# Token-major projections xv, hv and sv: from 1024 x 256 weight pieces to 512 x 512 pieces, in a fused two-block fp32 kernel

## The reference, cut to what matters

```python
# first block, cross-attention on the 256 memory rows
k, v = jnp.split(mem @ w_xkv, 2, axis=-1)          # xv: the v half, 1024 columns
o = jnp.einsum('bhsm,bmhd->bshd', pr, v)          # pr: softmax of q k, 4 heads of 256
# second block
proj = u @ w_in
hq, hf, hi, hg, sq, sk, sv = jnp.split(proj, splits, axis=-1)   # hv is hi, 512 columns; sv, 512 columns
o_hg = hgrn2_mix(hq, hf, hi, lb_all[i])                   # a decayed linear attention, hi as values
o_sb = stick_breaking_mix(sq, sk, sv)              # 8 heads of 64, sv as values
```

## Time and profile before

| | us |
|---|---|
| runs | 1045.93, 1047.46, 1048.79 (median 1047.46) |
| profiled execution, its own time | 1046.91 |
| its span in the trace | 1045.1 |
| PE busy | 990.6 |
| DVE busy | 626.1 |
| ACT busy | 514.2 |

### The profile page before, as it was taken

The page is one execution under the profiler, slowest core; times in us unless marked ns, Lnnn a source line. Parts: engine busy times, 40 slices in busy tenths (PEclk is TensorE's granted clock), DMA queues, the critical chain, the costliest instruction groups (busy, mean ns, idle before and its releaser), DMA issues.

```text
span 1045.1 us, 19430 instructions
## 1 busy us (share of the span) xinstructions
PE 990.6 (95%) x8574; PEld 914.9 (88%) x8574; DVE 626.1 (60%) x833; ACT 514.2 (49%) x693; POOL 19.6 (2%) x23
## 2 busy tenths in 40 slices
PE   7999999999999999999996777799999999999998
PEld 6999999899989999998674454499999999999998
DVE  6798789868676875444110110089984765555566
ACT  5576588834775573533111111177657554434453
POOL 0000021001000000000000000000000000000000
PEclk9999999999999999999998988899999999999999
DMA  7665453446235467788999999964421366455531
GB/s 290 243 236 183 187 190 134 161 162 224 99 125 206 154 220 279 316 353 334 423 418 421 420 420 421 419 221 162 162 82 52 124 242 239 168 196 202 200 124 42
DMA packets 34872, 241.76 MB, mean 231 GB/s; under 512 B 4064, under 2 KB 4448, under 8 KB 6368
## 3 DMA queue, kind: packets, MB, share of 16 engines
q1 hardware_dynamic: 33264, 233.32, 58.6%
q0 software_dynamic: 1232, 6.99, 1.8%
q10 hardware_dynamic: 288, 0.15, 0.1%
HBM read 239.36 MB, written 1.08 MB: 230 GB/s over the span
## 4 chain that ended last, share of the span: by engine, by line
PE 76%; DMA 12%; DVE 7%; ACT 2%; SPq 2%; issue 1%; DVEq 0%; ACTq 0%
PE ps L483 18%; PE ps L484 18%; PE ps L485 18%; DMA wr<-in_c_weights 8%; PE ps L572 3%; PE ps L1282 3%; DMA T8b<-in_c_weights 3%; SPq L3057 2%; DVE wlo L2048 2%; PE ps L969 1%; PE ps L1232 1%; DVE xs L2280 1%; ACT whi L1392 1%; PE ps L1309 1%; PE ps L856 1%
## 5 line engine op out<-in xcount | busy, mean ns | idle before, releaser
L2048 DVE TENSOR_TENSOR wlo<-raw,whi 128x2048 fp32r<-128x2048 f32 (+1 forms) x119 | 271.1, 2281 | 111.7 <-ACT whi L1392 111.3
L483 PE MATMUL ps<-XUh,whi 128*128 128x256 f32 x986 | 277.4, 281 | 0.5 <-DVE wlo L2048 0.4
L484 PE MATMUL ps<-XUl,whi 128*128 128x256 f32 x992 | 275.3, 277 | 0.0
L485 PE MATMUL ps<-XUh,wlo 128*128 128x256 f32 x992 | 274.9, 277 | 0.0
L1392 ACT ACTIVATE whi<-raw 128x2048 fp32r<-128x2048 f32 (+1 forms) x119 | 225.1, 1894 | 45.5 <-PE ps L485 39.0
L483 PEld LDWEIGHTS ps<-XUh,whi 128*128 128x128 f32 x986 | 185.5, 188 | 2.5 <-issue 1.7
L484 PEld LDWEIGHTS ps<-XUl,whi 128*128 128x128 f32 x992 | 186.6, 188 | 0.7 <-issue 0.5
L485 PEld LDWEIGHTS ps<-XUh,wlo 128*128 128x128 f32 x992 | 186.3, 188 | 0.0
L2980 DVE SCALAR_TENSOR_TENSOR sphs<-sphs,wsl,ps 128x256 f32<-128x256 f32 x8 | 3.8, 481 | 91.0 <-ACT sphs L2013 72.0
L483 PE MATMUL ps<-ffnah,whi 128*128 128x256 f32 x176 | 48.6, 276 | 0.0
L484 PE MATMUL ps<-ffnal,whi 128*128 128x256 f32 x176 | 48.6, 276 | 0.0
(11 more groups left out here) (626 smaller groups left out, 2377.9 us busy)
## 6 DMA issues: line engine op xcount, KB each, us to landing
raw<-in_c_weights SPq DMA_DIRECT2D x137, 1024.0 KB, 4.9
wr<-in_c_weights SPq DMA_DIRECT2D x36, 1024.0 KB, 26.1
xhi<-in_c_weights SPq DMA_DIRECT2D x12, 1024.0 KB, 26.2
xlo<-in_c_weights SPq DMA_DIRECT2D x12, 1024.0 KB, 26.4
extra<-in_c_weights SPq DMA_DIRECT2D x10, 1024.0 KB, 27.5
T<-in_c_weights SPq DMA_DIRECT2D x5, 1024.0 KB, 26.1
T8b<-in_c_weights SPq DMA_DIRECT2D x5, 1024.0 KB, 26.4
acb<-sums POOLq DMA_DIRECT2D x4, 1024.0 KB, 5.1
```

What stands on the lines that cost most here:

```text
L483: pe.matmul(ps, h(k), xh(k), start=start and k == 0, stop=False, skip_group_check=loose)
L484: pe.matmul(ps, h(k), xl(k), start=False, stop=False, skip_group_check=loose)
L485: t = pe.matmul(ps, l(k), xh(k), start=False, stop=stop and k == kt - 1, skip_group_check=loose)
L2048: dve.tensor_tensor(l[:, 0:n], r, h[:, 0:n].bitcast(F32), ALU.subtract).then_inc(*did("w_lo", "split", i))
```

## The change

`halved` makes pieces of 512 rows by 512 columns for xv, hv and sv; a piece is 1 MB as before, 4 row tiles of 128 x 512. Two pieces make one result of 512 columns. A product streams 512 columns. Each token tile has a bank of its own, which is held over both pieces; the first product of the even piece starts the sum and the last of the odd piece ends it. The two transposes ahead of xv are gone. ACT empties a pair of banks, 512 columns each, once the odd piece is through; for hv this is at the place of the old second `tokens`, and likewise for sv. In the second block hv and sv take banks 6 and 7 only, and scores, diagonal, z and rem rotate over banks 0 to 5 with a counter of their own, while sk, osb, oh, hg and the later users stay in the rotation over all eight.

```diff
@@ -183,6 +183,11 @@
         for c in range(c0, c0 + n, step):
             add(name, w, slice(c, c + step))
 
+    def halved(name, w, c0, n):
+        for c in range(c0, c0 + n, 512):
+            for k in (0, 512):
+                add(name, w[k:k + 512], slice(c, c + 512))
+
     w_in, w2, wgu, wdn = I["w_in"][0], I["w_in_2"][0], I["w_gate_up_2"][0], I["w_down_2"][0]
     add("dt", np.tile(w_in[:, 5120:5152], 4), slice(None))
     several("lora", w_in, 5152, 512)
@@ -205,7 +210,7 @@
     several("w_o", I["w_o"][0], 0, 1024)
     several("xk", I["w_xkv"][0], 0, 1024)
     several("xq", I["w_xq"][0], 0, 1024)
-    several("xv", I["w_xkv"][0], 1024, 1024)
+    halved("xv", I["w_xkv"][0], 1024, 1024)
     several("xo", I["w_xo"][0], 0, 1024)
 
     for g in range(8):
@@ -216,8 +221,8 @@
     several("hq", w2, 0, 512)
     several("sq", w2, 2048, 512)
     several("sk", w2, 2560, 512)
-    several("hv", w2, 1024, 512)
-    several("sv", w2, 3072, 512)
+    halved("hv", w2, 1024, 512)
+    halved("sv", w2, 3072, 512)
     several("hg", w2, 1536, 512)
     several("w_out2", I["w_out_2"][0], 0, 1024)
 
@@ -533,17 +538,19 @@
                     elif c == cs[0] and between is not None:
                         between()
 
-        def chunk_tok(name, c, xh, xl, kt, ready, banks=bank):
+        def chunk_tok(name, c, xh, xl, banks=bank, among=(0, 1, 2, 3, 4, 5, 6, 7)):
             i = first[name] + c
             h, l = split_of(i)
-            ps, free = banks.take(name, c)
-            w.wait_ge(*free)
+            if c % 2 == 0:
+                for j in range(2):
+                    _, free = banks.take(name, c // 2, j, among=among)
+                    w.wait_ge(*free)
             w.wait_ge(*at_("split", i))
-            if name == "xv" and c == 0:
-                lead_in(ps)
+            k0 = 4 * (c % 2)
             for j in range(2):
-                t = triple(ps[:, 256 * j:256 * j + 256], lambda k: xh[:, k, 128 * j:128 * j + 128], lambda k: xl[:, k, 128 * j:128 * j + 128],
-                           lambda k: h[:, k, :], lambda k: l[:, k, :], kt, ready)
+                f = slice(128 * j, 128 * j + 128)
+                t = triple(banks.ps(name, c // 2, j)[:, :], lambda k: xh[:, k0 + k, f], lambda k: xl[:, k0 + k, f],
+                           lambda k: h[:, k, :], lambda k: l[:, k, :], 4, start=k0 == 0, stop=k0 == 4)
             t.then_inc(*did("w_used", "used", i))
 
         def norm_sum(nm, nt, ng=1, banks=bank):
@@ -835,7 +842,7 @@
                 if r:
                     t.then_inc(*did("xa_pe", "xa_sc", j))
         for c in range(3):
-            chunk_tok("xv", c, MMh, MMl, 8, None)
+            chunk_tok("xv", c, MMh, MMl)
         for mj in range(2):
             for r in range(2):
                 ps, free = bank.take("xpT", mj, r)
@@ -845,12 +852,13 @@
                     for j in range(2):
                         t = pe.transpose(ps[:, 256 * a + 128 * j:256 * a + 128 * j + 128], Px[j][:, 2 * r + a, 128 * mj:128 * mj + 128], ident)
                 t.then_inc(*did("xa_pe", "xa_pT", mj, r))
-        chunk_tok("xv", 3, MMh, MMl, 8, None)
+        chunk_tok("xv", 3, MMh, MMl)
         for hd in range(4):
             ps, free = bank.take("xo_h", hd)
             w.wait_ge(*free)
             w.wait_ge(*at_("emptied", "xpT", 1, 1))
-            w.wait_ge(*at_("emptied", "xv", hd))
+            w.wait_ge(*at_("emptied", "xv", hd // 2, 0))
+            w.wait_ge(*at_("emptied", "xv", hd // 2, 1))
             for e in range(2):
                 for mj in range(2):
                     t = pe.matmul(ps[:, 256 * e:256 * e + 256], v2[:, mj, 256 * hd + 128 * e:256 * hd + 128 * e + 128], PXT[mj][:, hd, :],
@@ -955,14 +963,14 @@
             X = Xs[lv % 2]
             w.wait_ge(*at_("hg", "x", lv))
             if lv == 7:
-                ps, free = ebank.take("hsc", lv)
+                ps, free = ebank.take("hsc", lv, among=(0, 1, 2, 3, 4, 5))
                 w.wait_ge(*free)
                 for hd in range(4):
                     t = pe.matmul(ps[:, 128 * hd:128 * hd + 128], X[:, hd, 0:128], X[:, hd, 128:256])
                 t.then_inc(*did("hg_pe", "hsc", lv))
                 return
             for j in range(2):
-                ps, free = ebank.take("hsc", lv, j)
+                ps, free = ebank.take("hsc", lv, j, among=(0, 1, 2, 3, 4, 5))
                 w.wait_ge(*free)
                 for hd in range(4):
                     x = X[:, hd, 128 * j:128 * j + 128]
@@ -973,7 +981,7 @@
             w.wait_ge(*at_("hg", "k"))
             w.wait_ge(*at_("hq", "silu", 1))
             for j in range(2):
-                ps, free = ebank.take("hdiag", j)
+                ps, free = ebank.take("hdiag", j, among=(0, 1, 2, 3, 4, 5))
                 w.wait_ge(*free)
                 for hd in range(4):
                     t = pe.matmul(ps[:, 128 * hd:128 * hd + 128], hk[:, hd, 128 * j:128 * j + 128], hq[:, hd, 128 * j:128 * j + 128])
@@ -984,7 +992,8 @@
                 ps, free = ebank.take("oh", q)
                 w.wait_ge(*free)
                 w.wait_ge(*at_("emptied", "hsc", 7))
-                w.wait_ge(*at_("emptied", "hv", 1))
+                w.wait_ge(*at_("emptied", "hv", 0, 0))
+                w.wait_ge(*at_("emptied", "hv", 0, 1))
                 for r in range(2):
                     hd = 2 * q + r
                     d = ps[:, 256 * r:256 * r + 256]
@@ -998,7 +1007,7 @@
             for hl in range(4):
                 hd = 4 * g + hl
                 o, tl = 64 * (hd % 2), hd // 2
-                ps, free = ebank.take("sz", hd)
+                ps, free = ebank.take("sz", hd, among=(0, 1, 2, 3, 4, 5))
                 w.wait_ge(*free)
                 pe.matmul(ps[:, 0:256], sk[o:o + 64, tl, 0:128], sq[o:o + 64, tl, :])
                 pe.matmul(ps[:, 256:384], sk[o:o + 64, tl, 128:256], sq[o:o + 64, tl, 128:256]).then_inc(*did("sb_pe", "sz", hd))
@@ -1008,7 +1017,7 @@
             w.wait_ge(*at_("sb", "sp", g))
             for hl in range(4):
                 hd = 4 * g + hl
-                ps, free = ebank.take("srem", hd)
+                ps, free = ebank.take("srem", hd, among=(0, 1, 2, 3, 4, 5))
                 w.wait_ge(*free)
                 pe.matmul(ps[:, 0:256], tri, Sp[:, hl, 0:256], start=True, stop=False)
                 pe.matmul(ps[:, 128:256], ones[:, :], Sp[:, hl, 256:384], start=False, stop=True)
@@ -1019,7 +1028,8 @@
             ps, free = ebank.take("osb", g)
             w.wait_ge(*free)
             w.wait_ge(*at_("sb", "a", g))
-            w.wait_ge(*at_("emptied", "sv", 1))
+            w.wait_ge(*at_("emptied", "sv", 0, 0))
+            w.wait_ge(*at_("emptied", "sv", 0, 1))
             for hl in range(4):
                 hd = 4 * g + hl
                 o = 64 * (hl % 2)
@@ -1042,16 +1052,16 @@
         hgrn_scores(0)
         chunk("sk", 1, XUh, XUl, 8, None, banks=ebank)
         hgrn_scores(1)
-        chunk_tok("hv", 0, XUh, XUl, 8, None, banks=ebank)
+        chunk_tok("hv", 0, XUh, XUl, banks=ebank, among=(6, 7))
         hgrn_scores(2)
         stick_z(0)
-        chunk_tok("hv", 1, XUh, XUl, 8, None, banks=ebank)
+        chunk_tok("hv", 1, XUh, XUl, banks=ebank, among=(6, 7))
         hgrn_scores(3)
         stick_z(1)
-        chunk_tok("sv", 0, XUh, XUl, 8, None, banks=ebank)
+        chunk_tok("sv", 0, XUh, XUl, banks=ebank, among=(6, 7))
         hgrn_scores(4)
         stick_rem(0)
-        chunk_tok("sv", 1, XUh, XUl, 8, None, banks=ebank)
+        chunk_tok("sv", 1, XUh, XUl, banks=ebank, among=(6, 7))
         hgrn_scores(5)
         stick_rem(1)
         hgrn_scores(6)
@@ -1723,8 +1733,10 @@
             t.then_inc(*did("xa_act", "xa", "exp", j))
         for c in range(4):
             upcoming("xv", c)
-            w.wait_ge(*at_("used", first["xv"] + c))
-            copy(v2[:, :, 256 * c:256 * c + 256], halves(bank.ps("xv", c))).then_inc(*bank.emptied("xv", c))
+            if c % 2:
+                w.wait_ge(*at_("used", first["xv"] + c))
+                for j in range(2):
+                    copy(v2[:, j, 256 * c - 256:256 * c + 256], bank.ps("xv", c // 2, j)[:, :]).then_inc(*bank.emptied("xv", c // 2, j))
             if c == 2:
                 for mj in range(2):
                     for r in range(2):
@@ -1839,12 +1851,11 @@
             w.wait_ge(*at_("hg", "x_in", lv))
             act.activation(Xs[lv % 2][:, :, :], Xs[lv % 2][:, :, :], ACT.Exp).then_inc(*did("hg_act", "hg", "x_exp", lv))
 
-        def tokens(name, dst, c):
-            w.wait_ge(*at_("used", first[name] + c))
+        def tokens(name, dst):
+            w.wait_ge(*at_("used", first[name] + 1))
             w.wait_ge(*at_("emptied", "rcol"))
             for j in range(2):
-                t = copy(dst[:, j, 256 * c:256 * c + 256], ebank.ps(name, c)[:, 256 * j:256 * j + 256], scale=rcol[:, j:j + 1])
-            t.then_inc(*ebank.emptied(name, c))
```

(7 more changed lines are left out.)

## The result

The change makes the kernel slower. Its median is 1057.85 us in 6 runs (1052.77 to 1058.97), against 1049.30 in 6 of the kernel before (1045.93 to 1051.08): a ratio of **1.0085**, interval 1.0068 to 1.0101. The forecast was 1047.9, in a range up to 1051.0. The profiled execution took 1055.98 us with a span of 1054.2, which is 9.1 us more than the span before.

What follows compares the result with a forecast made beforehand. PE was taken to bound the kernel, so only a shorter PE stream or earlier expert stage wins time. Gain 3.8 less waits 4.2 gave net +0.4 us, a median of 1047.9, range 1044.3 to 1051.

Steps and rivals of the forecast that it cites:

- The pace of the products: xv, hv, sv: a 512-column product takes 216 ns against 236 for two old ones, gaining 3.8 us in all.
- 512 columns win nothing: Slower rival: xv, hv, sv products stay at 236 ns a pair, gain 0, time 1050.8 us; chance 0.08.
- Does that survive the expert stage?: Expert stage: its full DMA stretch starts and ends 1.9 us earlier, keeping xv's gain; bound 0 if loads lack time.
- The two transposes: Ahead of xv: they add 0.22 us, but their removal was costed at nothing, within 0.1.
- The four waits: Second block's bank order: PE waits 1.4 us before the diagonal, 1.9 before sv 0, nothing at spread(7), 0.9 before scores 7.
- the second wait: sv 0 after hv, both in banks 6 and 7: PE comes at 754.4, banks empty at 756.3, wait 1.9 us.
- This date stands: hv's eviction after level 5, done at 756.3, doesn't move because DVE has slack against PE.
- DMA and splits: Pieces keep bytes, order and buffers, and splits keep their size; cost nothing, covered by a piece's 5.2 us on PE.
- xv's evictions: After xv: ACT's copies end 1.1 us after the last piece, hidden behind 3.5 us of heads 0 and 1.
- the waits did come: Faster rival: the bank waits don't come and only the gain is left, 1043.7 us; chance 0.15.
- pace of later pieces: Slower rival: feed-forward products flip from 113 to 118 ns, costing 7 us, 1055 in all; chance 0.07.
- swallow xv's gain: Rival: the expert stage takes up xv's 1.9 us gain, giving 1049.8 us, inside 0.3%; chance 0.12.

Runs made afterwards that it cites:

- e6: e5 with sk 0, sk 1 and hg 0 also taking banks from the scores' six-bank rotation; 1052.57 us, ratio 1.0036 to the kernel before.
- e7: e6 plus 49 never-executed products in the branch not entered, restoring the old code length; 1048.29 us, ratio 1.0001 to the kernel before.
- e1: Changed kernel plus 49 never-executed products in the branch not entered, restoring the old code length; 1053.89 us, ratio 1.0056 to the kernel before.
- e4: Kernel before with only the hv, sv and bank part of the change; 1052.35 us, ratio 1.0045 to the kernel before.
- e5: Changed kernel with ACT's eviction of hv moved ahead of soft_z(0) and level 5; 1055.40 us, ratio 1.0062 to the kernel before.
- e8: Separate kernel computing nothing of the reference: trains of fp32r products at five widths, some behind plain fp32 products; ran once, 102.25 us.

## Why the prediction was wrong

**The pace of the products** failed in its size. It took 216 ns for 512 columns from L856's plain fp32 record, the wrong kind of product. The fp32r one takes 229, so a pair wins 7 ns and not 20, and the gain by that is 192 x 7 = 1.3 us, not 3.8. The mechanism (some cost beyond the columns, paid half as often) is right, but that cost isn't the same at both widths: with the columns at 0.42 ns each it is 11 ns of the 118, and 16 of the 229. The estimate from the Trainium skill (TensorE: Matmul & The Clock Gate, "Wait — 56ns, not 53.3ns?") that was set against it, 2.5 ns for each product saved and 0.5 us in all, was nearer in its sum. Its rule of N / 2.4 GHz + 2.5 ns gives 215.8 at 512 columns, where these fp32r products show 229. The rival "512 columns win nothing" was nearer than the forecast: the trace shows xv's products at -0.61, hv at -0.24 and sv 1 at -0.14, while sv 0's share is lost in the half clock.

**Does that survive the expert stage?** is the step that failed worst. It looked at the DMA only, and let PE's program be free. The 96 products that xv loses and the two transposes are also instructions (each with its weight load). Taking 196 out ahead of the stage moved a gap in PE's stream from behind product 48 of the last up products to behind product 17, where it is 3.1 us long instead of 0.4, and the clock is at half behind it. Gap and clock together cost 0.35% (e6 to e7), where the forecast had a gain of 1.9 us. The trace of before has both gaps (5.0 and 0.4 us of "issue"), but they weren't read. **The two transposes** had the price 0, within 0.1. Their removal won 0.22 us in xv, since the first product without them adds nothing extra, and they count as four instructions for the code's place.

**The four waits** came as forecast: 1.4, 1.9, nothing and 0.9 against 1.4 (1.8 in e1 and e4), 2.07, nothing and 0.9. For spread(7) the DVE's timeline after shows 1.61 us of idle ahead of L2740, for PE's scores (L977), so that it is still covered. e5 and e6 confirm the cause of the other three by removing them. The banks and releasers are right throughout. But the size of the second wait is in part luck, two misses that cancel. Put on the forecast's time scale (2.86 us earlier, what the diagonal was late by without its wait), PE arrived at 755.1 and not 754.4, since hv won only 0.24. And ACT was through with hv at 757.1 and not 756.3. "This date stands" failed: `spread(5)` and level 5 slipped with PE's delay, and the two copies took 1.25 us and not 1.1. With the date fixed and hv's real gain the wait would have been some 1.2 us.

**What the second wait leaves** was missing: no term for PE's clock. Seven products at half clock cost 1.5 us, seven tenths of the wait on top. The Trainium skill (TensorE: Matmul & The Clock Gate, "HAM oscillation — how this bites in real kernels") tells of products that restart at the lower clock after a wait between bursts, and the trace agrees in kind, though after a shorter wait than in the page's example: 0.43 us from start to start behind 2.07 us of waiting. The waits of 1.4 and 0.9 us, and that of 1.8 in e1 and e4, left the clock alone (1.00 in the 3 us behind each).

**DMA and splits, xv's evictions**: hidden, as forecast; xv is followed by L864 with no wait. **The rivals**: the waits did come, so no faster outcome. The pace of later pieces did not flip: xo takes 22.83 us before and after. In the feed-forward part, PE's timeline of the changed kernel has

```profile
867.08 0.28 PE L488 MATMUL ps<-ffnah,whi 128*128 128x256 f32 x1
...
868.78 0.28 PE L488 MATMUL ps<-ffnah,whi 128*128 128x256 f32 x1
```

with 15 products in 1.70 us, 113 ns as in the earlier trace rows. The expert stage did swallow xv's gain and more, but by PE's code and clock and not by the DMA, which the forecast's bound had named.

The median came out at 1057.85 where 1047.9 was forecast; 1.8 us of that is the kernel before itself, with 1049.30 in its six runs and not 1047.46. Set beside the ledger, the forecast of +0.4 us missed 8.7 us: expert stage 3.6, half clock at sv 1.5, the smaller gain of the projections 2.5 (xv 1.1, hv 0.7, sv 0.7), the longer second wait 0.2, and 0.9 after scores 7 in single executions, which in one kernel lie up to 6 us apart (1052.77 to 1058.97). This last part isn't explained.

**What stays open.** That the gap is a fetch, and that it is long because the instruction queue shares the DMA with a full weight stream (422 GB/s in that stretch), is argued from the place and the queue list alone. The runs show only that its place moves with the count of instructions and comes back after 256. Why it lasts 3 us behind product 17 and under 1.1 behind product 47 or 48 isn't known. Nor is what share of the 0.35% is gap and what is clock: each kernel has one trace, and the executions without a trace give only the mean clock. What picks 113 or 118 ns at 256 columns isn't known. e7 has a new wait of 0.4 us (scores 6 for DVE's `SC`), which may hide the gain of hv and sv (0.4 to 0.6 us); a rotation without it wasn't tried. No version here beats the kernel before.

## What to carry to other kernels

Cost a product by a row of its own type and width, or measure it first: the part beyond the columns was 11 ns at 256 columns and 16 at 512 here, so merging two products won only 2 x 11 - 16, about 7 ns. When a bank's life grows, write down the rotation and the eviction dates, which named every wait here, and ask of each date whether it moves when PE comes later. Look at the granted clock behind a wait: the one of 2.07 us cost 1.5 more. When PE's instruction count changes ahead of a stage that is bound by DMA, look for "issue" gaps in the trace and see where they fall afterwards and what the clock does behind them. A change of 0.3% may be no more than that, and shifting the code by never-executed instructions tells the two apart.

## What the runs showed of the hardware

- An fp32r product with a fresh 128 x 128 stationary tile starts every 228 ns at 512 columns, 174 at 384, 120 at 256 and 111 at 192 and 128 (e8); a plain fp32 record of 512 takes 216.
- Code that is never executed changes the time: 60 places +0.25% (0.07 to 0.44), 256 places 0.00%. A gap in PE's stream moves with it and is back after 256 places: behind product 47 or 48 of a group of 64 (0.4 to 1.1 us), or behind 17 or 18 (2.5 to 3.2 us).
- One wait of 2.07 us amid dense products was followed by 3.4 us at the lower clock in the changed kernel (0.52), and such a wait by a clock of 0.50 and 0.53 (757 to 760 us) in e1 and e4; e5, without the wait, kept 1.00. Waits of 0.9, 1.4 and 1.8 us were followed by 1.00.
